# A decode-step layer: the reversed bias table moved to its own home and stored first, the log-forget pages fetched as whole rows and turned on TensorE

## The reference

```python
def dilation_bias(rel_bias, window, dil):
    nk = window // dil
    return rel_bias[t5_bucket(dil * jnp.arange(nk + 1))]
...
    lf_all = jnp.concatenate([gather(cache_lf).astype(jnp.float32), logf], axis=1)
    cum = jnp.cumsum(lf_all, axis=1)
```

## Time and profile before

| | us |
|---|---|
| median of 3 runs | 2771.72 (2769.49 to 2774.2) |
| the profiled execution | 2768.85 |
| span of its profile | 2766.8 |
| PE busy (matmul), share of the span | 2482.3, 90% |
| DVE busy | 1148.8, 42% |
| ACT busy | 908.4, 33% |
| POOL busy | 44.6, 2% |
| mean granted TensorE clock | 0.95 |

### The profile page before, as it was taken

One profiled execution on the slowest core, in us unless ns is written; L12 is line 12 of the kernel. 1 busy time (PEld: TensorE's weight loads), 2 busy tenths in 40 slices (PEclk: granted clock), 3 DMA queues, 4 the chain that ended last, 5 costly groups with the idle time before them and its releaser, 6 DMA issues.

```text
span 2766.8 us, 51111 instructions
## 1 busy us (share of the span) xinstructions
PE 2482.3 (90%) x20799; PEld 2298.1 (83%) x20799; DVE 1148.8 (42%) x1725; ACT 908.4 (33%) x1113; POOL 44.6 (2%) x86
## 2 busy tenths in 40 slices
PE   6602999999999999989999877788999999999999
PEld 3301999999999999979999543478999999999999
DVE  0300344443444444566664111245444544444444
ACT  1300333223332333366653111234433333333332
POOL 0130000000000000000000000000000000000000
PEclk8755999999999999999999998999999999999999
DMA  8506777777776775434455899964444544454444
GB/s 343 236 3 182 283 307 282 286 309 262 308 282 235 301 273 204 161 122 152 152 186 200 325 385 372 408 247 136 140 166 164 168 167 167 158 163 168 166 166 155
DMA packets 105919, 614.93 MB, mean 222 GB/s; under 512 B 16192, under 2 KB 16464, under 8 KB 56128
## 3 DMA queue, kind: packets, MB, share of 16 engines
q1 hardware_dynamic: 101728, 603.81, 59.0%
q0 software_dynamic: 4064, 9.26, 1.4%
HBM read 604.36 MB, written 8.66 MB: 222 GB/s over the span
## 4 chain that ended last, share of the span: by engine, by line
PE 82%; DMA 8%; issue 3%; SPq 2%; POOLq 2%; DVE 1%; ACT 1%; POOL 0%; ACTq 0%; DVEq 0%
PE banks L591 25%; PE banks L590 25%; PE banks L592 24%; PE banks L618 4%; DMA adax<-in_w_ada_dram 2%; DMA rev_dram<-rev 1%; SPq L468 1%; POOLq L495 1%; PE banks L874 1%; DMA kv_h<-in_vpool_dram 1%; DMA kv_raw<-in_wink_dram 1%; DMA kv_z<-in_wink_dram 1%; PE banks L831 1%; SPq L459 1%; PE banks L693 1%
## 5 line engine op out<-in xcount | busy, mean ns | idle before, releaser
L590 PE MATMUL banks<-h_hi,w_hi 128*128 128x288 f32 x3792 | 1124.4, 297 | 38.9 <-DVE h_lo L1171 22.8
L591 PE MATMUL banks<-h_lo,w_hi 128*128 128x288 f32 x3792 | 1122.4, 296 | 0.0
L592 PE MATMUL banks<-h_hi,w_lo 128*128 128x288 f32 x3792 | 1121.3, 296 | 0.0
L1139 DVE TENSOR_TENSOR w_lo<-raw,w_hi 128x1024 fp32r<-128x1024 f32 (+2 forms) x666 | 763.5, 1188 | 605.1 <-ACT w_hi L911 598.7
L911 ACT ACTIVATE w_hi<-raw 128x1024 fp32r<-128x1024 f32 (+2 forms) x666 | 672.5, 1032 | 844.3 <-PE banks L592 577.6
L590 PEld LDWEIGHTS banks<-h_hi,w_hi 128*128 128x128 f32 x3792 | 716.9, 189 | 52.6 <-issue 46.8
L591 PEld LDWEIGHTS banks<-h_lo,w_hi 128*128 128x128 f32 x3792 | 716.8, 189 | 0.8
L592 PEld LDWEIGHTS banks<-h_hi,w_lo 128*128 128x128 f32 x3792 | 716.1, 189 | 0.0
L590 PE MATMUL banks<-g_hi,w_hi 128*128 128x288 f32 x1376 | 407.8, 296 | 0.0
L591 PE MATMUL banks<-g_lo,w_hi 128*128 128x288 f32 x1376 | 406.8, 296 | 0.0
L592 PE MATMUL banks<-g_hi,w_lo 128*128 128x288 f32 x1376 | 406.6, 296 | 0.0
(11 more groups left out here) (191 smaller groups left out, 1127.6 us busy)
## 6 DMA issues: line engine op xcount, KB each, us to landing
raw<-in_w_dram SPq DMA_DIRECT2D x172, 1024.0 KB, 4.9
adaw<-in_w_ada_dram SPq DMA_DIRECT2D x56, 1024.0 KB, 6.7
adaw_b<-in_w_ada_dram SPq DMA_DIRECT2D x56, 1024.0 KB, 11.0
raw<-in_w_dram SPq DMA_DIRECT2D x64, 896.0 KB, 4.6
raw<-in_w_in_dram SPq DMA_DIRECT2D x49, 1024.0 KB, 4.8
adax<-in_w_ada_dram SPq DMA_DIRECT2D x32, 1024.0 KB, 8.0
raw<-in_w_dram SPq DMA_DIRECT2D x32, 960.0 KB, 4.8
raw<-in_w_out_dram SPq DMA_DIRECT2D x16, 1024.0 KB, 4.9
```

The costliest lines, as they stand in the source:

```text
L590: pe.matmul(bank[:, 0:T], hi, m_hi[:, k, :], start=k == 0, stop=False)
L591: pe.matmul(bank[:, 0:T], hi, m_lo[:, k, :], start=False, stop=False)
L592: last = pe.matmul(bank[:, 0:T], lo, m_hi[:, k, :], start=False, stop=k == nk - 1)
L1139: dve.tensor_tensor(w_lo[:, r, a:b], raw[:, r, a:b], w_hi[:, r, a:b].bitcast(F32), ALU.subtract).then_inc(S["lo_ready"], 1)
```

## The change

`rev` gets memory of its own, at the start of `v_new`, which the kernel first uses at the end of the mixing layer's projections. SP's first batch no longer waits for `rev_stored`. POOL stores `rev` as soon as it is there, ahead of everything else but the first four loads, and waits for that store. Then it fetches the 64 pages, each as one row of 4 KB into one partition of `lfrow` (on the same memory as `rev`), with the loop written out; `big` and `rbr` follow. After the second segment of `ffn1` (the first `down`), PE turns `lfrow` into `lfc`'s shape with 8 transposes of 64 x 128, one for each head, into bank 5 (`turn_log_forget`), and DVE copies them into `lfc`. DVE's later wait for `lf_landed` becomes one for that copy.

```diff
--- before.py
+++ after.py
@@ -200,8 +200,6 @@
         sq_sum = at("sq_sum", [P, T], F32, sq0 + T * 4)
 
         y0, ms, tt = (at(n, [P, T], F32, sq0 + k * T * 4) for k, n in enumerate(("y0", "ms", "tt")))
-        rev = at("rev", [HEADS, REV], F32, sq0 + 3 * T * 4)
-
         fa_sb, fe = at("fa_sb", [HEADS, T], F32, sq0 + 5 * T * 4), at("fe", [HEADS, T], F32, sq0 + 6 * T * 4)
         adax = at("adax", [P, 4, KT * P], F32, mix0)
         assert 4 * KT * P * 4 <= 2 * 15 * T * 4
@@ -212,6 +210,8 @@
         rbr = sb("rbr", [P, HEADS])
         v_new = sb("v_new", [TS, 2 * HEADS * HD])
         vn0 = top[0] - 2 * HEADS * HD * 4
+        rev = at("rev", [HEADS, REV], F32, vn0)
+        lfrow = at("lfrow", [NB * PAGES, PAGE * HEADS], F32, vn0)
         ohr = at("ohr", [32, REV], F32, vn0 + 4096)
         adr = at("adr", [HEADS, REV], F32, vn0 + 5632)
 
@@ -277,7 +277,7 @@
         names = """ld_small ld_x w_landed0 w_landed1 hi_ready lo_ready w_used acc_a_read acc_b_read ada_landed0
             ada_landed1 ada_landed2 ada_landed3 adax_landed0 adax_landed1 adax_landed2 adax_landed3 ada_used ada_sb ada_sel ada_fin
             c_ready sq_ready sq_used y0_ready hf_ready hhi_ready hn_ready gain_ready h_ready g_ready
-            act_chain dve_chain y_stored heads_stored v_stored ss_read ld_att ld_rel ld_selw ld_pages
+            lfc_sum lfc_ready act_chain dve_chain y_stored heads_stored v_stored ss_read ld_att ld_rel ld_selw ld_pages
             lf_landed rev_sum rev_ready rev_stored toe_landed fa_ready fe_ready lf_ready hsq_ready hss_ready
             hy_ready head_ready lft_sum lft_ready ncum_sum ncum_ready p_s p_max p_exp p_scaled p_v p_vcopy
             p_t p_tcopy p_o p_high p_low vn_sum vn_ready kv_landed0 kv_landed1 kv_landed2 kv_first_landed
@@ -413,7 +413,6 @@
                     sp.wait_ge(S["ada_used"], 2 * KT + t)
                     if t == 0:
                         sp.wait_ge(S["h_ready"], SQR)
-                        sp.wait_ge(S["rev_stored"], 16)
                 for j in (2 * part, 2 * part + 1):
                     sp.dma_start(adaq[j], w_ada[2 * KT + 2 * (t // 2 * 4 + j) + t % 2, :, :])\
                       .then_inc(S[f"ada_landed{j}"], 16)
@@ -486,18 +485,17 @@
             pool.dma_start(rbs[:, :], relb).then_inc(S["ld_rel"], 16)
             pool.dma_start(ohr[:, :], ohrev).then_inc(S["ld_rel"], 16)
             pool.dma_start(adr[:, :], addrev).then_inc(S["ld_rel"], 16)
-            pool.wait_ge(S["h_ready"], 1)
+            pool.wait_ge(S["rev_ready"], 1)
+            pool.dma_start(rev_dram, rev[:, :].unsqueeze(1).to_broadcast([HEADS, P, REV])).then_inc(S["rev_stored"], 16)
+            pool.wait_ge(S["rev_stored"], 16)
+            pool.wait_ge(S["ld_pages"], 16)
+            for i in range(NB * PAGES):
+                pg = pool.value_load(pages[0:1, i:i + 1], min_val=0, max_val=POOL - 1)
+                pool.dma_start(lfrow[i:i + 1, :], lfpool[bass.ds(pg, 1), :, :].rearrange("a p h -> a (p h)"))\
+                    .then_inc(S["lf_landed"], 16)
             pool.dma_start(big[:, :], cst2).then_inc(S["ld_att"], 16)
             for q in range(NS):
                 pool.dma_start(rbr[32 * q:32 * q + 32, :], relb).then_inc(S["ld_att"], 16)
-            pool.wait_ge(S["ld_pages"], 16)
-            with pool.Fori(0, NB * PAGES) as i:
-                pg = pool.value_load(pages[0:1, bass.ds(i, 1)], min_val=0, max_val=POOL - 1)
-                pool.dma_start(lfc[:, bass.ds(i, 1), :], lfpool[bass.ds(pg, 1), :, :].rearrange("a p h -> p a h"))\
-                    .then_inc(S["lf_landed"], 16)
-            pool.wait_ge(S["rev_ready"], 1)
-            pool.dma_start(rev_dram, rev[:, :].unsqueeze(1).to_broadcast([HEADS, P, REV])).then_inc(S["rev_stored"], 16)
-            pool.wait_ge(S["rev_stored"], 16)
             pool.wait_ge(S["h_ready"], 2 * SQR)
             pool.dma_start(selw[:, :], selh).then_inc(S["ld_selw"], 16)
 
@@ -681,6 +679,17 @@
                         run(seg, pe, lambda i, seg=seg: pair(seg, i), 1)
                     if seg.squares:
                         sum_squares(seg)
+                    if seg is ffn1[1]:
+                        turn_log_forget()
+
+            def turn_log_forget():
+
+                pe.wait_ge(S["lf_landed"], 16 * NB * PAGES)
+                rows = lfrow[:, :].rearrange("a (p h) -> a p h", h=HEADS)
+                for h in range(HEADS):
+                    last = pe.transpose(bank[5][:, h * NB * PAGES:(h + 1) * NB * PAGES], rows[:, :, h],
+                                        ident[0:NB * PAGES, 0:NB * PAGES])
+                last.then_inc(S["lfc_sum"], 1)
 
             segments(ffn1)
 
@@ -1307,6 +1316,10 @@
                     else:
                         run(seg, dve, lambda i, seg=seg: body(seg, i, (seg, i - 1)), 1, ch, LINKS[seg.kind])
                     late = seg, seg.bodies - 1
+                    if seg is ffn1[1]:
+                        dve.wait_ge(S["lfc_sum"], 1)
+                        dve.tensor_copy(lfc[:, :, :].rearrange("p a h -> p h a"),
+                                        bank[5].rearrange("p (h a) -> p h a", h=HEADS)).then_inc(S["lfc_ready"], 1)
                 r = 1 if seg in ffn1 else 2
                 if seg.squares:
                     splits(split_low, r, -2)
@@ -1409,7 +1422,7 @@
                 p_low(t)
 
 
-            dve.wait_ge(S["lf_landed"], 16 * NB * PAGES)
+            dve.wait_ge(S["lfc_ready"], 1)
             dve.wait_ge(S["lft_ready"], 1)
             dve.tensor_copy(lfn_w[:, :].rearrange("p (j h q) -> p j h q", j=GB, q=NS),
                             lft[0:TS, 2, :].unsqueeze(1).unsqueeze(3).to_broadcast([TS, GB, HEADS, NS]))
```

## The result

The changed kernel takes **2674.34 us** (median of 4 runs, 2673.55 to 2675.6) against 2771.74 before (4 runs on the same chip): a ratio of 0.9649, 95% interval 0.9632 to 0.9666, 97.4 us less. The forecast was 2680, with 91 us. That the sum came so near is in part luck: two of its terms missed in opposite directions.

What follows compares the result with a forecast made beforehand. The prediction took SP's wait for the bias table's store, which held the weight stream, as the bound. 119.7 us won, less 25 for the store and 3.4 for the turn, gave 91 us: 2680 us, range 2656 to 2694.

Steps and rivals of the forecast that it cites:

- What bounds the kernel: Before the first `w_ada` batch, PE waits 128.3 us because SP's queue stands 148.1 us on the bias table's store.
- The wait taken away, 119.7 us: SP issues its first weight batch at 123.1 us instead of 242.8, 119.7 us earlier.
- The store beside the weights, 25 us given back: The store, on 8 wholly busy engines, delays the first two waves of weights: 20 us plus 5 us.
- the first wave: First batch, 32 packets per engine: 4 pass before the store's data, the other 28 wait 0.71 us each, 20 us.
- The second wave, 5 us of the 25: Two tiles of the next batch and a weight tile: the store's last 7 packets per engine cost 5 us.
- One for one: On a shared DMA engine, store and weight queues alternate packet by packet, so weights lose 0.71 us with each store packet.
- The signs: Named beforehand: PE's wait before line 618 falls from 128.3 to about 28 us; under 18 or over 35 means wrong.
- weights hardly hindered: Rival: the store keeps 16 engines half busy or takes gaps; 12 us given back, 2667 us (2655 to 2674); chance 0.28.
- The turn, 3.4 us: After the first `down` segment, PE's transposes, DVE's copy, half a split and handovers cost 3.4 us, once.
- Pages at 1.51 us each and `big` at nothing: On POOL after the store, 64 pages at 1.51 us each end before needed; `big` fits beside the weights.
- the slower rival: PE's turn after the first `down` segment waits for the pages; from 6.5 us a page the kernel is slower; chance 0.02.
- After the second wave transfers have slack: Past the first two waves of weights, transfers have slack and PE is the bound again.

Runs made afterwards that it cites:

- Wait only: Kernel before, with only the bias table in its own home and SP's wait for the store removed; old pages, no turn: 2665.9 us.
- Store from 16: Changed kernel with the bias table on 16 partitions, each head's row twice, instead of 8: 2662.4 us.
- store later: Changed kernel with POOL's store held until PE has used five weight tiles: 2668.1 us.
- store from 128: Changed kernel with the bias table made on 128 partitions, 16 for each head, each storing 8 copies of its row: 2663.3 us.
- change, store in mix: Changed kernel with the store moved to the start of the mixing layer: 2674.0 us.
- wait only, store in mix: Kernel before with the table in its own home, SP's wait removed and the store moved to the mixing layer's start: 2670.3 us.

## Why the prediction was right, and where not

- **What bounds the kernel** (the wait in SP's program): right. Wait only, two lines, moves the first waves from 150.2 to 32.75.
- **The wait taken away, 119.7 us**: right. Kernels whose store is elsewhere have first waves of 30.4 and 31.5 us (pages as rows) or 32.3 to 32.75 (old pages): 117.5 to 119.8 us less than 150.2.
- **The store beside the weights, 25 us given back**: mis-sized. It is 46.7 - 31 = 16 us, where 31 is the mean of the two kernels with the same pages and the store elsewhere. The reading of 8 engines was right (0.51 while weights still move; 35.6 to 20.3 us of landing when 16 take part). The step that failed is the first wave, "the other 28 wait 28 x 0.71 = 20 us"; both factors were too large. By 131 us, when the store's data has barely begun, 1.77 MB of the batch had moved, 216 rows of 8 KB or 13.5 of each engine's 32, where the prediction let 4 through: the store's data came more than 4 us behind the batch's and not 1. And a weight packet lost less than 0.71 us with each packet of the store: between 140 and 152 us the weights moved 0.95 MB, 116 rows on 8 engines, one every 0.83 us on each, so each loses 0.83 - 0.31 = 0.52 us. That gives 18.5 x 0.52 = 9.6 us (an estimate from these rows); measured is 22.0 - 12.5 = 9.5. In those 12 us the store sent 0.56 MB, some 122 packets of 4.6 KB, in 31.4% of 16 engines, which is 0.49 us each, less than the 0.71 that they took alone. Why they are shorter there, the runs don't show.
- **The second wave, 5 us of the 25**: near, by another mechanism. From PE's start on the batch to the landing of the second wave's weight tile it takes 158.52 + 10.99 - 146.82 = 22.7 us, before 262.41 + 8.97 - 255.26 = 16.1, so 6.6 more. One for one was right for the first wave (some 116 packets against 122) but not here: between 158 and 160 us the store's queue moves 21 packets and the weights' 3.
- **The store's landing of 48 us**: wrong for the same reason. It lands in 35.6 us beside the weights and in 33.8 alone: its packets hardly wait for those of the weights.
- **The signs.** PE's wait before the first batch is 18.2 us where about 28 was named; under 18 would have counted against the mechanism, so it held by a hair.
- **The rival "weights hardly hindered"**, 12 us and 2667: nearer in size than the forecast's 25, wrong in its mechanism. The measured 2674.3 lies at the border that the prediction drew between the two cases.
- **The turn, 3.4 us**: right in sum, with the copy at 1.07 instead of 0.7 us and 1.09 for the transposes. Store from 16 shows it bare: 3.4. Not forecast was the clock, most of the other 6.4 - 3.4 = 3.0 us: from PE's start at 487.6 until 493.5 us products come every 0.24 us instead of 0.13, which is about 2.6 us lost (an estimate). It falls in four of the five kernels that keep the copy's place: for some 7 us in both runs of the change, for some 3.5 in store later, store from 128 and change, store in mix, whose second stage also starts some 2 us longer at the low clock. "Bounds: 1.2 to 7 us" held it, for another reason.
- **Pages at 1.51 us each and `big` at nothing**: they now take 1.14 us from one to the next (the first at 162.91, the last at 234.7), and neither is seen in a wait; no wait for the pages, so the slower rival has nothing for it.
- **"After the second wave transfers have slack"**: wrong for this store. In the changed kernel it doesn't matter, since the store has landed by then; in store later and wait only it costs 6.5 and 9.3 us.

Together: 119.7 - 25 - 3.4 = 91 was forecast; 119.3 - 16 - 6.4 = 97 is what the stages give, and 97.4 the medians. The store was 9 us too dear and the seam 3 us too cheap; that the sum missed by 6 and not by 9 is luck.

## What to carry to other kernels

A wait that holds the whole weight stream is worth what the chain of waits says, and it can be won alone: here two lines did it, while the rest of the change gave some of it back. Before a small store is moved, see how many partitions it leaves from: this one, from 8 rows, kept 8 engines busy and landed in 34 to 36 us wherever it was put, and the weights beside it were as late as those 8 engines let them be, so spread it over all partitions first and then put it where transfers have slack and not where the first weights are awaited. An operation added to an engine that feeds PE goes behind the work that PE waits for next.

## What the runs showed of the hardware

- A store packet and a weight packet on one DMA engine, 0.71 and 0.31 us alone, together took about 0.83 us (140 to 152 us in the changed kernel), and the store was hardly slower for it (35.6 against 33.8 us). In wait only, store in mix the weights first stood: from 1109 to 1113 us no packet of theirs moved, and a tile issued into the running store landed in 24.1 us instead of 4.8.
- The same pause of PE, 2.3 us at the same place, was followed by a fall of the granted clock from 1.00 to 0.50 in the changed kernel (486.7 to 493.5 us), by one of half that length in three others (from 483.0 to 486.5 us in store from 128) and by none in the store from 16 (1.00 throughout). What decides it, these runs don't show; in the changed kernel the fall costs about 2.6 us (estimate above).
- The same 1.5 MB to the same rows of DRAM land, beside weights, in 34.7 to 36.4 us from 8 partitions, 20.3 from 16 and 16.4 to 18.4 from 128, and cost PE 9 us or nothing in the same stage. The Trainium skill, "DMA: Bandwidth & Descriptors", warns of an outer dimension under 16 under "Rules for kernel authors"; the numbers agree. From 128 partitions the packets were cheaper still than from 16 (10.2% of the engines against 21.4% in the same 41 us).
